# Layer 1's adaLN columns: weight tiles summed on VectorE in place of skinny matmuls on TensorE, in a two-layer trunk

## The chip, the cores and the metric

One core of a Trainium2 chip runs the whole program in one launch. The metric is the device time in microseconds (us) of one execution; lower is better. TensorE (PE in the profile) does the matmuls and transposes, VectorE (DVE) and ScalarE (ACT) the elementwise work, GpSimd (POOL) some of it, and SyncE (SP) issues the weight transfers.

## What is computed

A two-layer encoder trunk over 256 tokens of width 1024, in float32. Layer 0 is a pooling and S5 mixer, then a dense SwiGLU of hidden width 2816; layer 1 is a Mamba-2 mixer, then a top-2-of-8 expert SwiGLU. Each of the four sub-layers is framed by a modulation that comes from one conditioning vector c:

```
for layer in range(DEPTH):
    mod = (jax.nn.silu(c) @ ada_w[layer] + ada_b[layer])[:, None, :]
    sh_m, sc_m, g_m, sh_f, sc_f, g_f = jnp.split(mod, 6, axis=-1)
    h = _modulate(x, norm_g[layer, 0], sh_m, sc_m)
...
        y = _mamba2_mixer(h, m2_w_in[i], ...)
    x = x + g_m * _rmsnorm(y, norm_g[layer, 1])
    h = _modulate(x, norm_g[layer, 2], sh_f, sc_f)
...
```

`ada_w[layer]` is 1024x6144, so `silu(c) @ ada_w[layer]` is a product of one row with a 24 MB matrix, once per layer.

## The kernel before

**Tiles and order.** All weights stream through a ring of seven 2 MB slots, filled by SP in one fixed order (`plan`, L49) and freed by a counter, `tile_used`, that TensorE raises after the last use of each tile, in that same order. Each layer's `ada_w` is cut into 12 tiles (`NADA`) of 1024x512, held as 128 partitions x 8 chunks x 512 columns. Layer 0's twelve are used at the head of the program, layer 1's twelve are spread through the dense SwiGLU of layer 0.

**One ada tile before.** `ada_mm` (L1251) multiplies the eight chunks of the tile with the eight columns of silu(c) (`cT`) as 32-column weights, two chunks into each of four partition groups of bank 6; ScalarE's `ada` (L552) copies that bank to `modparts`; `ada_turn` (L1262) transposes it in four 128-column pieces into bank 7; VectorE's `mods` (L797) reduces the four groups and adds the bias, giving four columns of `mod`. So a tile goes TensorE, ScalarE, TensorE, VectorE, with one copy buffer and one bank at each step.

**The dense SwiGLU** (L1438 to L1465, and L674 and L972 on ScalarE and VectorE) runs six steps t. In step t TensorE computes, for each of four (two in the last step) groups of 128 hidden columns, a gate chain into bank 4 and an up chain into bank 5 of eight matmuls each; ScalarE takes silu of bank 4, VectorE multiplies it with bank 5 (`f_act`, L979). The next up chain may only start when that product has left bank 5. Then `ffn_down` of step t-1 adds into banks 0 to 3. Ada tiles are placed around these:

```
                if t < 5:
                    ada_turn(NADA + 2 * t + 1)
                pe.wait_ge(s["f_mm"], 8 * t + 2 * n_f)
                pe.sem_inc(s["tile_used"], 2)
                if t < 4:
                    ada_mm(NADA + 2 * t + 2)
                if t:
                    ffn_down(t - 1)
                if t < 4:
                    ada_turn(NADA + 2 * t + 2)
                    ada_mm(NADA + 2 * t + 3)
```

Tiles 0 and 1 of layer 1 are multiplied before the SwiGLU, between the end of the mixer's output projection and `turn_x(2)` (L1415 to L1419), tiles 10 and 11 behind it, before `turn_x(3)` (L1466 to L1473). These two places are boundaries between sub-layers: ScalarE squares the outputs (`y_squares`), VectorE forms the residual (`residual`) and the normalised x (`norm_x`), TensorE transposes it (`turn_x`, L1270), ScalarE and VectorE apply shift and scale (`hT_high`, `hT_low`), and the first chain of the next stage (`first_chain`, L1243) starts. At another such boundary, before the router, sixteen 128-column products of the identity (`stay_warm`, L1237) stand ahead of `turn_x(4)`. The first stage of layer 1 begins with one chain of eight matmuls and then 16 matmuls of only 32 columns (`dtw`, L1508).

Of the kernel before, what the change touches and what calls it, by code (L numbers as in the profile page):

```python
# [13 lines left out]
ALU = mybir.AluOpType  # L14
ACT = mybir.ActivationFunctionType
# [4 lines left out]
P = 128  # L20
D = 1024
KC = D // P
# [3 lines left out]
HALF = 512  # L26
# [22 lines left out]
def plan():  # L49

    tiles = []

    def put(kind, n, slot):
        tiles.append((kind, n, slot))

    head = [("ada0", n) for n in range(4)] + [("mixin", 1), ("mixin", 0)]
    head += [("ada0", n) for n in range(4, NADA)] + [("glu", 0), ("mixout", 0), ("mixout", 1)]
    for n, (kind, i) in enumerate(head):
        put(kind, i, n % S5_SLOTS)

    ada = [("ada1", n) for n in range(NADA)]
    ffn = ada[:2]
    for t in range(6):
        ffn += [("gate", t), ("up", t)]
        if t < 4:
            ffn.append(ada[2 * t + 2])
        if t:
            ffn.append(("down", t - 1))
        if t < 4:
            ffn.append(ada[2 * t + 3])  # L70
    ffn += [("down", 5)] + ada[10:]
    for n, (kind, i) in enumerate(ffn):
# [37 lines left out]
def hybrid_trunk(nc, a, out):  # L110
    with ExitStack() as ctx:
# [70 lines left out]
        def norm_col(layer, i):  # L182
# [20 lines left out]
        modparts = area(13312, HALF), area(18944, HALF)  # L203
# [60 lines left out]
            ada_copied ada_turned mod_ready inv_ready band_ready  # L264
# [276 lines left out]
        def _(act):  # L541
# [10 lines left out]
            def ada(i):  # L552

                act.wait_ge(s["tile_used"], ADA[i] + 1)
                if i:
                    act.wait_ge(s["ada_turned"], i)
                c.inc(f(modparts[i // NADA], ps[6][:, :], ACT.Copy), "ada_copied")
# [110 lines left out]
            ada(NADA)  # L668
            squares(1)
            ada(NADA + 1)  # L670
# [3 lines left out]
            for t in range(6):  # L674
                for j in range(2 if t == 5 else 4):
                    n = 4 * t + j
                    act.wait_ge(s["f_mm"], 2 * n + 1)
                    if n >= 2:
                        act.wait_ge(s["f_act"], n - 1)
                    c.inc(f(silu_f[:, n % 2], ps[4][:, 0:TOK], ACT.Silu), "f_silu")  # L680
                if t < 4:
                    ada(NADA + 2 * t + 2)
                    ada(NADA + 2 * t + 3)
            grow_rows(2, grow)
            y_squares(2)
            ada(2 * NADA - 2)
# [3 lines left out]
            ada(2 * NADA - 1)  # L690
            hT_high(3, NADA + 10, mod[:, 1, 0])
# [55 lines left out]
            hT_high(4, 2 * NADA, mod[:, 1, 3], hT2)  # L747
# [40 lines left out]
        def _(dve):  # L788
# [8 lines left out]
            def mods(i):  # L797

                dve.wait_ge(s["ada_turned"], i + 1)
                m = modraw[:, i % 2]  # L800
                c.then(v.tensor_reduce(m, bank(7, 4, 4, 32)[:, :, :, 0], AX.X, ALU.add), step)
                layer, n = i // NADA, i % NADA
                at = layer * 48 + 4 * n
                c.inc(tt(mod_flat[:, at:at + 4], m, cols[:, 0, at:at + 4], ALU.add), "mod_ready")

# [160 lines left out]
            mods(NADA)  # L966
# [21 lines left out]
            mods(2 * NADA - 2)  # L988
            scale_cols(3, NADA + 10, mod[:, 1, 1], norm_col(1, 0))
            hT_low(3, mod[:, 1, 0])  # L990
            mods(2 * NADA - 1)
# [95 lines left out]
            scale_cols(4, 2 * NADA, mod[:, 1, 4], norm_col(1, 2))  # L1087
# [135 lines left out]
        def _(pe):  # L1223
# [38 lines left out]
            def ada_turn(i):  # L1262
# [3 lines left out]
                for k in range(4):  # L1266
                    ins = turn(ps[7][:, P * k:P * k + P], modparts[i // NADA][:, P * k:P * k + P], ident[:, :])
# [147 lines left out]
            ada_mm(NADA)  # L1415
            ada_turn(NADA)
            ada_mm(NADA + 1)
# [20 lines left out]
            for t in range(6):  # L1438
# [20 lines left out]
                if t < 4:  # L1459
                    ada_turn(NADA + 2 * t + 2)  # L1460
                    ada_mm(NADA + 2 * t + 3)
# [4 lines left out]
            ada_mm(2 * NADA - 2)  # L1466
            ada_turn(2 * NADA - 2)
            ada_mm(2 * NADA - 1)
# [4 lines left out]
            ada_turn(2 * NADA - 1)  # L1473
# [19 lines left out]
            for n in range(32):  # L1493
# [10 lines left out]
                if n == 0:  # L1504
                    pe.wait_ge(s["l1_in"], 96)
                    pe.wait_ge(s["ada_copied"], 2 * NADA)
# [19 lines left out]
            pe.wait_ge(s["mod_ready"], 2 * NADA)  # L1526
# [267 lines left out]
```

## Time and profile before

| | us |
|---|---|
| median of 3 runs | 1730.05 |
| lowest and highest | 1729.53, 1731.7 |
| the profiled execution | 1730.87 |
| its span | 1729.0 |
| TensorE busy in it | 1563.1 |
| VectorE busy in it | 389.0 |
| granted TensorE clock, mean | 0.972 of full speed |

The span is the time from the first to the last instruction of the profiled execution; its own time is 1.9 us longer. "Granted clock" is the share of TensorE's full speed that the chip gave; it has two levels, 1.00 (2.4 GHz) and 0.50 (1.2 GHz).

The order of the main stages in the span: the layer 0 mixer ends at 201 us, the dense SwiGLU runs from 209.6 to 461 us, the Mamba-2 stage starts at 470 us, the experts fill the last 930 us.

### The profile page before, as it was taken

To read this page: it belongs to the slowest core of one execution; us is meant where nothing else is said; L and a number is where in the kernel's file an instruction comes from. 1 tells how busy PE (TensorE), PEld (TensorE's weight loads), DVE (VectorE), ACT (ScalarE), POOL (GpSimd) and SP (SyncE) were. 2 spreads that over 40 slices of the span, in tenths; PEclk is the share of its full clock that TensorE was granted. 3 is DMA by queue.
4 is the path that set the end of the run, shared out by engine and by line. 5 is a ranking of instruction groups with operands and counts; after the bars stand their busy time and mean duration, and the time that the engine had idled before them with its cause. 6 is when DMAs were issued, how large, how long until landed. Compare 5 with 4: busy or idle time off the path is not lost.

```text
span 1729.0 us, 24503 instructions
## 1 busy us (share of the span) xinstructions
PE 1563.1 (90%) x10777; PEld 898.4 (52%) x10778; DVE 389.0 (23%) x846; ACT 219.7 (13%) x419; POOL 106.3 (6%) x129
## 2 busy tenths in 40 slices
PE   7886999999999999988999999999979979877876
PEld 5654486667588766554333353356646643423322
DVE  5796200000255555131010001010010010100102
ACT  2411300000321143220000000000000000000001
POOL 6164000000000011000000000000000000000000
PEclk8998999999999999988999999999989989999999
DMA  9476396642464404434999887999979969999996
GB/s 335 160 245 245 143 352 257 241 171 100 164 226 147 146 1 147 146 146 167 404 409 409 314 292 305 403 408 407 403 270 371 378 249 402 405 409 403 408 408 245
DMA packets 167299, 485.78 MB, mean 281 GB/s; under 512 B 12928, under 2 KB 15872, under 8 KB 167168
## 3 DMA queue, kind: packets, MB, share of 16 engines
q1 hardware_dynamic: 162624, 482.51, 73.4%
q8 instruction: 106, 1.74, 0.4%
q10 hardware_dynamic: 4544, 1.33, 0.4%
q14 instruction: 25, 0.20, 0.0%
HBM read 482.78 MB, written 1.05 MB: 280 GB/s over the span
## 4 chain that ended last, share of the span: by engine, by line
PE 73%; DMA 11%; DVE 6%; issue 5%; SPq 3%; ACT 1%; POOL 0%; DVEq 0%; POOLq 0%; ACTq 0%
PE bank L1694 23%; PE bank L1234 20%; PE bank L1725 10%; DMA ring<-in_moe_w_down 7%; PE bank L1429 4%; PE bank L1619 3%; DMA ring<-in_moe_w_up 3%; SPq L439 3%; PE bank L1539 2%; PE bank L1671 2%; DMA ring<-in_moe_w_gate 1%; PE bank L1259 1%; DVE arena L941 1%; PE bank L1241 1%; PE bank L1578 1%
## 5 line engine op out<-in xcount | busy, mean ns | idle before, releaser
L1694 PE MATMUL bank<-ring,arena 128*32 128x256 f32 (+3 forms) x4864 | 506.5, 428 | 72.9 <-issue 45.7
L1694 PEld LDWEIGHTS bank<-ring,arena 128*32 128x32 f32 (+1 forms) x4864 | 231.3, 121 | 337.1 <-issue 262.8
L1234 PE MATMUL bank<-arena,ring 128*128 128x256 f32 x1264 | 283.8, 384 | 1.3 <-ACT arena L646 1.0
L1725 PE MATMUL bank<-ring,arena 128*32 128x256 f32 (+1 forms) x2128 | 249.9, 459 | 29.9 <-DMA ring<-in_moe_w_down 27.6
L1234 PEld LDWEIGHTS bank<-arena,ring 128*128 128x128 f32 x1264 | 241.2, 193 | 38.9 <-issue 4.5
L1725 PEld LDWEIGHTS bank<-ring,arena 128*32 128x32 f32 (+1 forms) x2128 | 101.6, 120 | 168.1 <-issue 118.6
L1159 DVE TENSOR_TENSOR arena<-arena,bank 128x512 f32<-128x512 f32 (+2 forms) x44 | 24.4, 577 | 606.8 <-PE bank L1694 606.8
L763 ACT ACTIVATE arena<-bank 128x512 f32<-128x512 f32 (+2 forms) x44 | 21.1, 508 | 692.3 <-PE bank L1706 576.0
L1429 PE MATMUL bank<-ring,arena 128*128 128x512 f32 x176 | 77.0, 595 | 0.3 <-PE bank L1234 0.3
L1539 PE MATMUL bank<-ring,arena 128*128 128x512 f32 x128 | 59.3, 606 | 2.5 <-DVE hd L1055 2.5
L1619 PE MATMUL bank<-ring,arena 128*128 128x512 f32 x128 | 55.3, 592 | 0.0
L1429 PEld LDWEIGHTS bank<-ring,arena 128*128 128x128 f32 x176 | 33.0, 190 | 42.5 <-issue 42.4
L1259 PE MATMUL bank<-ring,cT 128*32 128x512 f32 x384 | 48.0, 618 | 3.1 <-DMA ring<-in_ada_w 2.5
L1173 DVE TENSOR_TENSOR arena<-arena,bank 128x512 f32<-128x512 f32 x32 | 22.0, 688 | 108.7 <-PE bank L1671 107.9
L979 DVE TENSOR_TENSOR arena<-arena,bank 128x256 f32<-128x256 f32 x22 | 9.3, 422 | 164.4 <-PE bank L1234 164.4
L503 POOL TENSOR_TENSOR arena<-arena,ring 128x512 f32<-128x512 f32 x32 | 41.5, 1316 | 70.1 <-DVE arena L949 62.8
L1145 DVE TENSOR_SCALAR arena<-bank,gs,mod 128x128 f32<-128x128 f32 x64 | 21.9, 404 | 95.5 <-PE bank L1234 95.5
L528 POOL COPY arena<-arena 128x6 f32<-128x6 f32 x8 | 1.5, 190 | 669.2 <-DVE arena L1136 649.2
L1234 PE MATMUL bank<-ring,arena 128*128 128x512 f32 x96 | 42.0, 594 | 0.1
L518 POOL TENSOR_TENSOR arena<-arena,hd 128x256 f32<-128x256 f32 x16 | 10.2, 638 | 515.9 <-ACT arena L700 388.2
L1619 PEld LDWEIGHTS bank<-ring,arena 128*128 128x128 f32 x128 | 24.2, 190 | 29.7 <-issue 29.7
L1539 PEld LDWEIGHTS bank<-ring,arena 128*128 128x128 f32 x128 | 23.7, 196 | 26.8 <-issue 26.8
(262 smaller groups left out, 1122.9 us busy)
## 6 DMA issues: line engine op xcount, KB each, us to landing
ring<-in_moe_w_gate SPq DMA_DIRECT2D x56, 2048.0 KB, 21.5
ring<-in_moe_w_up SPq DMA_DIRECT2D x56, 2048.0 KB, 22.3
ring<-in_moe_w_down SPq DMA_DIRECT2D x56, 2048.0 KB, 19.3
ring<-in_ada_w SPq DMA_DIRECT2D x24, 2048.0 KB, 11.1
ring<-in_m_w_in SPq DMA_DIRECT2D x12, 2048.0 KB, 8.5
ring<-in_ffn_w_gate SPq DMA_DIRECT2D x5, 2048.0 KB, 16.5
ring<-in_ffn_w_up SPq DMA_DIRECT2D x5, 2048.0 KB, 12.4
ring<-in_ffn_w_down SPq DMA_DIRECT2D x5, 2048.0 KB, 7.9
```

The source lines that it names most:

```text
L439: sp.dma_start(dst, src.rearrange("e p k n -> p (e k) n")).then_inc(ring_full[j % RING], 16)
L503: c.inc(g.tensor_tensor(qq[:, q % 2, k], zz[:, q % 2], tables[:, 1 - k, q:q + 1, :].broadcast_to([P, 2, TOK]), ALU.mult), "q_ready")
L1159: ins = tt(sg[:, b, 0:w], sg[:, b, 0:w], ps[2 + b][:, 0:w], ALU.mult)
L1173: tt(o, o, ps[SCATTER[i]][:, :], ALU.add).then_inc(s["acc_done"], 1)
L1234: ins = mm(out_, l, r, start=i == 0, stop=i == len(pairs) - 1, **kw)
L1259: ins = mm(ps[6][32 * j:32 * j + 32, :], cT[:, kc, :], w[:, kc, :], start=half == 0, stop=half == 1)
L1429: ins = mm(ps[i][:, :], act_f[:, t % 2, j, P * b:P * b + P], w[:, j, HALF * h:HALF * h + HALF], start=t == 0 and j == 0, stop=t == 5 and j ...
L1539: ins = mm(ps[6 + zi % 2][:, :], hT[:, kc, P * b:P * b + P], w[:, kc], start=kc == 0, stop=kc == KC - 1)
L1619: ins = mm(ps[4 + i][:, :], yT1[:, 4 * t + j, P * b:P * b + P], w[:, j, HALF * h:HALF * h + HALF], start=t == 0 and j == 0, stop=t == 3 an ...
L1671: mm(ps[SCATTER[i]][:, :], gates[:, P * (i // 2):P * (i // 2) + P], y_sb[:, HALF * (i % 2):HALF * (i % 2) + HALF], start=True, stop=True). ...
L1694: ins = mm(ps[base + b // per][m * h:m * h + m, w * (b % per):w * (b % per) + w], hcur3[:, kc, m * b:m * b + m], sl[:, kc - half * rows, w ...
L1725: ins = mm(ps[4 + b // per][m * h:m * h + m, w * (b % per):w * (b % per) + w], actT[:, t % 2, b // per, n * (b % per) + i, m * q:m * q + m ...
```

## The change

Layer 1's twelve ada tiles no longer go through `ada_mm` and `ada_turn`. VectorE forms, for each tile, the sum over its eight chunks of the chunk times its column of silu(c) (one `tensor_scalar` and seven `scalar_tensor_tensor` operations over 128x512, each waiting for the one before) into one of two buffers, `modsum`. TensorE sums that over the partitions with four matmuls per tile, each with 128 columns of `modsum` as weights and one column of ones as the moving operand, into four columns of bank 7, and frees the tile. After the twelfth tile VectorE adds the bias to all 48 columns at once. ScalarE has no part in it any more. All twelve tiles now lie inside the six steps of the SwiGLU, two per step, and the load order is changed to fit.

```diff
-    ffn = ada[:2]
+    ffn = []
     for t in range(6):
-        ffn += [("gate", t), ("up", t)]
-        if t < 4:
-            ffn.append(ada[2 * t + 2])
+        ffn += [("gate", t), ("up", t), ada[2 * t]]
         if t:
             ffn.append(("down", t - 1))
-        if t < 4:
-            ffn.append(ada[2 * t + 3])
-    ffn += [("down", 5)] + ada[10:]
+        ffn.append(ada[2 * t + 1])
+    ffn.append(("down", 5))
...
+            def sum_rows(n, first):
+
+                o = modsum[:, n % 2]
+                i = AT["ada1", n]
+                w = slot(TILES[i][2], KC, HALF)
+                if first == 0:
+                    dve.wait_ge(ring_full[TILES[i][2]], 16 * FILL[i])
+                    if n >= 2:
+                        dve.wait_ge(s["tile_used"], AT["ada1", n - 2] + 1)
+                for kc in range(first, first + 4):
+                    if kc == 0:
+                        c.then(ts(o, w[:, 0], cT[:, 0, 0:1], None, ALU.mult), step)
+                    else:
+                        c.then(stt(o, w[:, kc], cT[:, kc, 0:1], o, ALU.mult, ALU.add),
+                               "ada_summed" if kc == KC - 1 else step)
...
                     c.inc(tt(act_f[:, t % 2, j], silu_f[:, n % 2], ps[5][:, 0:TOK], ALU.mult), "f_act")
-                if t < 5:
-                    mods(NADA + 2 * t + 1)
-                if t < 4:
-                    mods(NADA + 2 * t + 2)
+                    if t < 5:
+                        sum_rows(2 * t + j // 2, 4 * (j % 2))
+                    else:
+                        sum_rows(10, 4 * j)
+            sum_rows(11, 0)
+            sum_rows(11, 4)
+            dve.wait_ge(s["tile_used"], AT["ada1", NADA - 1] + 1)
+            c.inc(tt(mod_flat[:, 48:96], ps[7][:, 0:48], cols[:, 0, 48:96], ALU.add), "mod_ready")
             residual(2, 12, 2, grow)
...
-            ada_mm(NADA)
-            ada_turn(NADA)
-            ada_mm(NADA + 1)
+            def ada_columns(n):
+
+                pe.wait_ge(s["ada_summed"], n + 1)
+                for k in range(4):
+                    ins = mm(ps[7][:, 4 * n + k:4 * n + k + 1], modsum[:, n % 2, P * k:P * k + P], ones[:, 0:1],
+                             start=True, stop=True)
+                ins.then_inc(s["tile_used"], 1)
...
-                if t < 5:
-                    ada_turn(NADA + 2 * t + 1)
                 pe.wait_ge(s["f_mm"], 8 * t + 2 * n_f)
                 pe.sem_inc(s["tile_used"], 2)
-                if t < 4:
-                    ada_mm(NADA + 2 * t + 2)
+                ada_columns(2 * t)
                 if t:
                     ffn_down(t - 1)
-                if t < 4:
-                    ada_turn(NADA + 2 * t + 2)
-                    ada_mm(NADA + 2 * t + 3)
+                ada_columns(2 * t + 1)
...
             ffn_down(5)
-            ada_mm(2 * NADA - 2)
-            ada_turn(2 * NADA - 2)
-            ada_mm(2 * NADA - 1)
 
             pe.wait_ge(s["x_ready"], 4)
             turn_x(3)
-            ada_turn(2 * NADA - 1)
```

ScalarE loses its `ada` copies of layer 1, and the waits on `mod_ready` behind the SwiGLU now wait for the one addition.

TensorE, from the mixer's output projection (L1234 before, L1242 now, 128x512 x32) to the third step of the SwiGLU; `first_chain` is L1248 before and L1256 now, `turn_x` L1275 and L1283, gate and up chains the 128x256 rows, `ffn_down` L1429 and L1442. Before:

```order
L1234 MATMUL bank<-ring,arena 128x512 x32
L1259 MATMUL bank<-ring,cT 32x512 x8
L1267 MATMUL bank<-ident,arena 128x128 x4
L1259 MATMUL bank<-ring,cT 32x512 x8
L1275 MATMUL bank<-ident,arena 128x128 x16
L1248 MATMUL bank<-arena,ring 128x256 x8
L1234 MATMUL bank<-arena,ring 128x256 x56
L1267 MATMUL bank<-ident,arena 128x128 x4
L1259 MATMUL bank<-ring,cT 32x512 x8
L1267 MATMUL bank<-ident,arena 128x128 x4
L1259 MATMUL bank<-ring,cT 32x512 x8
L1234 MATMUL bank<-arena,ring 128x256 x64
```

And now, with `ada_columns` at L1427:

```order
L1242 MATMUL bank<-ring,arena 128x512 x32
L1283 MATMUL bank<-ident,arena 128x128 x16
L1256 MATMUL bank<-arena,ring 128x256 x8
L1242 MATMUL bank<-arena,ring 128x256 x56
L1427 MATMUL bank<-ones,arena 128x1 x8
L1242 MATMUL bank<-arena,ring 128x256 x64
L1427 MATMUL bank<-ones,arena 128x1 x4
L1442 MATMUL bank<-ring,arena 128x512 x16
L1427 MATMUL bank<-ones,arena 128x1 x4
```

Nothing stands between the projection and `turn_x` any more, and the eight one-column matmuls of the first step (two tiles) follow each other directly.

VectorE in the last step of the SwiGLU, now; L985 is the product `f_act`, L808 and L810 are `sum_rows`, L993 the addition of the bias, L848 the start of the residual:

```order
L985 TENSOR_TENSOR arena<-arena,bank 128x256
L808 TENSOR_SCALAR arena<-ring,cT 128x512
L810 SCALAR_TENSOR_TENSOR arena<-ring,cT,arena 128x512 x3
L985 TENSOR_TENSOR arena<-arena,bank 128x256
L810 SCALAR_TENSOR_TENSOR arena<-ring,cT,arena 128x512 x4
L808 TENSOR_SCALAR arena<-ring,cT 128x512
L810 SCALAR_TENSOR_TENSOR arena<-ring,cT,arena 128x512 x7
L993 TENSOR_TENSOR mod<-bank,cols 128x48
L848 TENSOR_TENSOR arena<-bank,arena 128x512 x3
```

The second half of tile 10's sum stands behind the last product, and tile 11's whole sum behind that; in every other step one half of a sum stands behind each product.

## Rows read from the trace of the kernel before

**Rows 1.** The page: busy us, share of the span and instructions.

```profile
PE 1563.1 (90%) x10777; PEld 898.4 (52%) x10778; DVE 389.0 (23%) x846; ACT 219.7 (13%) x419; POOL 106.3 (6%) x129
```

**Rows 2.** The chain that ended last, in the SwiGLU: start us, us, what.

```profile
213.31 24.17 PE bank L1234 x112
...
243.00 27.82 PE bank L1234 x128
...
273.12 13.93 PE bank L1429 x32
...
382.01 27.82 PE bank L1234 x128
410.27 13.84 PE bank L1429 x32
424.11 13.83 PE bank L1234 x64
438.23 13.97 PE bank L1429 x32
```

**Rows 3.** The timeline at the mixer's end, ScalarE: start us, us, instruction, idle before.

```profile
203.18 0.60 ACT L557 ACTIVATE arena<-bank 128x512 f32<-128x512 f32 x1 [1.03 <-PE bank L1259]
...
203.84 1.06 ACT L564 ACTIVATE arena<-x 128x1024 f32<-128x1024 f32 x1
```

**Rows 4.** The timeline of VectorE: a product, then scalar_tensor_tensor pairs of two widths.

```profile
237.52 0.42 DVE L979 TENSOR_TENSOR arena<-arena,bank 128x256 f32<-128x256 f32 x1 [6.49 <-PE bank L1234]
...
462.48 2.48 DVE L849 SCALAR_TENSOR_TENSOR x<-arena,rst,x 128x1024 f32<-128x1024 f32 x2
...
481.05 1.00 DVE L1017 SCALAR_TENSOR_TENSOR arena<-bank,cols,arena 128x255 f32<-128x255 f32 x2
```

**Rows 5.** Groups by line and shape, VectorE: count | busy us, mean ns.

```profile
L1027 DVE TENSOR_TENSOR arena<-arena 128x512 f32<-128x512 f32 x16 | 10.9, 680 | 0.0
```

**Rows 6.** The timeline of TensorE: 32-column products, chains, and turn_x at two places.

```profile
206.52 2.30 PE L1275 MATMUL bank<-ident,arena 128*128 128x128 f32 x16 [0.17 <-DVE arena L811]
...
473.67 3.74 PE L1234 MATMUL bank<-dtw,arena 128*128 128x32 f32 x32
477.22 8.77 PE L1234 MATMUL bank<-arena,ring 128*128 128x256 f32 x32
...
486.05 3.62 PE L1234 MATMUL bank<-arena,ring 128*128 128x256 f32 x16
...
763.63 3.49 PE L1275 MATMUL bank<-ident,arena 128*128 128x128 f32 x16 [2.96 <-DVE arena L811]
```

**Rows 7.** Stretches: length, PE, PEld, DVE, ACT, POOL busy (count), granted clock, DMA, GB/s.

```profile
115.30:118.70 3.40, 1.54 (x12) 0.68 (x4) 3.33 (x7) 0.60 (x1) 1.68 (x2) 1.00 1.04 389
118.70:122.10 3.40, 3.00 (x9) 2.60 (x10) 3.30 (x6) 0.00 (x0) 2.19 (x3) 0.50 1.05 393
...
147.70:151.00 3.30, 0.00 (x0) 0.01 (x1) 3.23 (x7) 0.60 (x1) 1.63 (x3) 1.00 0.55 204
151.00:156.20 5.20, 2.42 (x12) 1.73 (x12) 5.06 (x10) 0.42 (x1) 3.12 (x3) 1.00 0.00 0
156.30:166.40 10.10, 6.76 (x16) 4.91 (x16) 1.93 (x4) 2.08 (x3) 1.90 (x2) 0.50 0.80 280
201.20:206.50 5.30, 4.43 (x36) 1.32 (x37) 4.23 (x7) 3.91 (x10) 0.00 (x0) 1.00 0.82 279
461.20:466.40 5.20, 4.39 (x36) 1.26 (x36) 4.23 (x7) 3.81 (x10) 0.00 (x0) 1.00 0.84 275
473.70:477.10 3.40, 3.40 (x33) 3.40 (x31) 0.00 (x0) 0.00 (x0) 0.00 (x0) 1.00 1.05 385
477.10:480.50 3.40, 3.40 (x10) 2.77 (x10) 1.04 (x6) 2.42 (x4) 0.00 (x0) 0.50 1.05 388
...
763.90:767.10 3.20, 3.20 (x16) 2.81 (x14) 0.51 (x2) 0.00 (x0) 0.00 (x0) 0.50 1.03 417
```

**Rows 8.** SP's timeline, then the DMA issues of 100 to 480 us with median landing.

```profile
201.43 3.85 SPq L404 DMA_DIRECT2D ring<-in_ada_w  x2
...
ring<-in_ada_w SPq DMA_DIRECT2D x15, 2048.0 KB, 12.8
```

More of the change, by code:

```diff
@@ L202, in hybrid_trunk @@
         grow = area(13312, D)
-        modparts = area(13312, HALF), area(18944, HALF)
+        modpart = area(13312, HALF)
+        modsum = area(8192, 2, HALF)
         temps = area(14336, 2, 2, 2, TOK)
@@ L263, in hybrid_trunk @@
         names = """small_in x_in step_in s5_in c_in pw_in l1_in consts t_iota rows_turned cols_ready cT_zero c_ready
-            ada_copied ada_turned mod_ready inv_ready band_ready
+            ada_copied ada_turned ada_summed mod_ready inv_ready band_ready
             step_exp step_ready mag_ready inv_tail turn_ready turn_sin tab_ready tab_sin bx_zero bx_ready b_turned bt_ready c_turned ct_zero ct_ready
@@ L556, in ada @@
                     act.wait_ge(s["ada_turned"], i)
-                c.inc(f(modparts[i // NADA], ps[6][:, :], ACT.Copy), "ada_copied")
+                c.inc(f(modpart, ps[6][:, :], ACT.Copy), "ada_copied")
             def squares(n):
@@ L667, in _ @@
             y_squares(1)
-            ada(NADA)
             squares(1)
-            ada(NADA + 1)
             hT_high(2, NADA, mod[:, 0, 3])
@@ L680, in _ @@
                     c.inc(f(silu_f[:, n % 2], ps[4][:, 0:TOK], ACT.Silu), "f_silu")
-                if t < 4:
-                    ada(NADA + 2 * t + 2)
-                    ada(NADA + 2 * t + 3)
             grow_rows(2, grow)
             y_squares(2)
-            ada(2 * NADA - 2)
             squares(2)
-            ada(2 * NADA - 1)
-            hT_high(3, NADA + 10, mod[:, 1, 0])
+            hT_high(3, NADA + 1, mod[:, 1, 0])
             act.wait_ge(s["l1_in"], 96)
@@ L746, in _ @@
             squares(3)
-            hT_high(4, 2 * NADA, mod[:, 1, 3], hT2)
+            hT_high(4, NADA + 1, mod[:, 1, 3], hT2)
             act.wait_ge(s["rt_pre"], 1)
@@ L965, in _ @@
             norm_x(2)
-            mods(NADA)
             scale_cols(2, NADA, mod[:, 0, 4], norm_col(0, 2))
@@ L979, in _ @@
                     c.inc(tt(act_f[:, t % 2, j], silu_f[:, n % 2], ps[5][:, 0:TOK], ALU.mult), "f_act")
-                if t < 5:
-                    mods(NADA + 2 * t + 1)
-                if t < 4:
-                    mods(NADA + 2 * t + 2)
+                    if t < 5:
[6 more added lines that the diff above has]
+            c.inc(tt(mod_flat[:, 48:96], ps[7][:, 0:48], cols[:, 0, 48:96], ALU.add), "mod_ready")
             residual(2, 12, 2, grow)
             norm_x(3)
-            mods(2 * NADA - 2)
-            scale_cols(3, NADA + 10, mod[:, 1, 1], norm_col(1, 0))
+            scale_cols(3, NADA + 1, mod[:, 1, 1], norm_col(1, 0))
             hT_low(3, mod[:, 1, 0])
-            mods(2 * NADA - 1)
             gate_cols(3, mod[:, 1, 2], norm_col(1, 1))
@@ L1084, in _ @@
             residual(3, 20, 4, grow1, 4, True)
-            scale_cols(4, 2 * NADA, mod[:, 1, 4], norm_col(1, 2))
+            scale_cols(4, NADA + 1, mod[:, 1, 4], norm_col(1, 2))
             norm_x(4)
@@ L1266, in ada_turn @@
                 for k in range(4):
-                    ins = turn(ps[7][:, P * k:P * k + P], modparts[i // NADA][:, P * k:P * k + P], ident[:, :])
+                    ins = turn(ps[7][:, P * k:P * k + P], modpart[:, P * k:P * k + P], ident[:, :])
                 ins.then_inc(s["ada_turned"], 1)
@@ L1450, in _ @@
                         ins.then_inc(s["f_mm"], 1)
-                if t < 5:
-                    ada_turn(NADA + 2 * t + 1)
                 pe.wait_ge(s["f_mm"], 8 * t + 2 * n_f)
                 pe.sem_inc(s["tile_used"], 2)
-                if t < 4:
-                    ada_mm(NADA + 2 * t + 2)
+                ada_columns(2 * t)
                 if t:
                     ffn_down(t - 1)
-                if t < 4:
-                    ada_turn(NADA + 2 * t + 2)
-                    ada_mm(NADA + 2 * t + 3)
+                ada_columns(2 * t + 1)
             pe.wait_ge(s["gg_ready"], 2)
@@ L1505, in _ @@
                     pe.wait_ge(s["l1_in"], 96)
-                    pe.wait_ge(s["ada_copied"], 2 * NADA)
+                    pe.wait_ge(s["ada_copied"], NADA)
                     for b in range(NB):
@@ L1524, in _ @@
                     ins.then_inc(s["cs_mm"], 1)
-            pe.wait_ge(s["mod_ready"], 2 * NADA)
+            pe.wait_ge(s["mod_ready"], NADA + 1)
             def z_part(n):
```

## The prediction

> **What bounds the kernel now.** I read the page first: TensorE is busy 90% of the span, VectorE 23% [rows 1]. Then the chain that ended last, since busy shares say nothing of a stage. Inside the dense SwiGLU that chain is TensorE alone: chains, down products and, between them, the ada work, each starting where the last ends [rows 2]. So there an ada tile costs what it takes on TensorE, and VectorE has long idle stretches (6.49 us before each product [rows 4]). At the two boundaries around the SwiGLU the chain runs through ScalarE and VectorE instead, and TensorE's ada work fits in their shadow. Last I read the granted clock in short stretches, because the change takes work off TensorE exactly where it is not the bound [rows 7].
>
> After the SwiGLU everything is shifted by whatever is gained or lost: the ring is only seven tiles deep and SP loads in order, so the experts' transfers start later or earlier by the same amount. I carry the sum unchanged to the end.
>
> **The sum with the clock at full speed.** Price of a one-column set: four matmuls, two passes each in float32. The nearest row is the 32-column product, 32 passes in 3.55 us from 473.67 to 477.22 [rows 6], 0.111 us a pass, bound by loading 128 columns of weights: 8 x 0.111 = 0.89 us. Bounds: 0.8 to 1.0.
>
> Price of one step of the sum on VectorE, 128x512: two 1024-column operations take 2.48 us together, two 255-column ones 1.00 [rows 4], so 1.24 and 0.50 per step are the ends; a two-source 512-column operation takes 0.680 [rows 5]. I take 0.72 with the wait for the step before. Half a tile is then 2.9 us. It fits the 6.49 us idle behind each product, so the next product, and TensorE's next up chain, are not late; it would take 1.6 us a step for that.
>
> - *Step 0.* Before, the chain ends at 213.31 + 24.17 = 237.48 and the next starts at 243.00 [rows 2]: 5.52 us for two turns, two ada products and a wait for ScalarE's copy. Now tile 0's columns (0.89) run while VectorE finishes tile 1, whose second half stands behind the product: 0.46 for the product, 2.88 for four steps, 0.1 for the signal, then 0.89: 4.3 us. Gain 1.2.
> - *Steps 1 to 3.* Before, 243.00 + 27.82 = 270.82 to 273.12 [rows 2], 2.3 us, six times. Now 0.89 six times; the sum behind `ffn_down` is long done (13.9 us cover it). Gain 6 x 1.41 = 8.4.
> - *Step 4.* Before, 409.83 to 410.27, 0.44 us, and nothing at 424.11 [rows 2]. Now two sets, 1.78. Loss 1.3.
> - *Step 5.* Before, 437.94 to 438.23, 0.29 us [rows 2]. Now TensorE waits for tile 10's second half, which stands behind the last product: 0.46 + 2.88 + 0.1 + 0.89 = 4.3. Loss 4.0. Tile 11 is summed under `ffn_down(4)`; its columns cost 0.9.
> - *Boundaries.* ScalarE's copy ended at 203.78 and its squares began at 203.84, when the residual's first half was just ready [rows 3]; removing the copy is worth at most 0.06. The other pieces lie under the transposes. Gain 0.
> - *Loads.* The order is gate 0, up 0, ada 0 into the three slots free early, then ada 1, issued near 201.4 where two ada tiles are issued now [rows 8]. It is wanted by VectorE at about 231; even at twice the 12.8 us to landing [rows 8] it is there. Later tiles have more time. Cost 0. VectorE waiting for a tile would hold the product queued behind it and so TensorE; that is a rival.
> - *The bias* is added under the last down products; the residual follows later. Cost 0.
>
> Sum: -1.2 - 8.4 + 1.3 + 4.0 + 0.9 = **-3.4 us**.
>
> **The clock.** Today TensorE is busy 4.43 of 5.30 us at the first boundary and 4.39 of 5.20 at the second, and the clock stays at 1.00 [rows 7]. Most of that is the ada work; without it TensorE stands idle for over 5 us at each. What such idling does is shown elsewhere: 3.30 idle us from 147.7 were followed by thin work at 1.00 and then by 10.1 us at 0.50; a stretch of 3.40 us with TensorE busy 1.54 was enough for 0.50 in the next [rows 7]. And thin matmuls don't hold it: TensorE was busy all of 473.7 to 477.1 with 32-column products, and had 0.50 from 477.1 [rows 6, 7]. So I expect it to fall at both boundaries, and at the two new waits (steps 0 and 5), where for over 4 us there is nothing but waiting and one-column matmuls.
>
> Prices: `turn_x` takes 3.49 us at 0.50 against 2.30 at 1.00 [rows 6]: 1.2, all on the chain. Chains: 32 passes across the half-speed stretch took 8.77 us, where 16 take 3.62 and the next 16 add about 3.5: 1.7 lost [rows 6].
> - First boundary: 1.2 plus a little of the first chain, 1.4.
> - Second: the same 1.2, but the fall at 477.1 is paid already, and the new one may replace or precede it: 0.6 (ends 0 and 2.9).
> - Each wait: up to 1.7 on the chains behind it, and the one-column matmuls slower, 0.9 at most; 2.0 each, 4.0.
>
> That is +6.0, and the whole **+2.6 us**: 1730.87 for the profiled execution becomes 1733.5. That execution lies 0.8 above the median of the runs, 1730.05, so the median becomes **1732.6**. The ends: all stays at full speed, -3.4; or every fall costs both turns and chains, below.
>
> The Trainium skill, page "TensorE: Matmul & The Clock Gate", section "Why this matters for your kernels", advises against idle gaps between bursts of matmuls because the engine drops back to half clock. By that rule the change gives back its gain, sum +2.6; without it the sum is -3.4. The trace agrees where it shows such gaps (0.50 after the stretches above).
>
> **Rivals.**
> *A. The clock holds.* The idling at the boundaries doesn't pull it down, or the half-speed stretch falls into the wait itself, where it costs nothing. For it: after 147.7 to 151.0, wholly idle, the clock stayed at 1.00 for 5.2 us more [rows 7]. Against it: it then fell. Time: 1730.05 - 3.4 = 1726.7. Chance 0.15.
> *B. Half speed lasts.* At each of the four places the clock comes back only after more than one stretch, as after 156.3 (10.1 us at 0.50 with TensorE busy 6.76 [rows 7]). Each boundary then costs 1.2 + 1.7 and each wait 0.9 + 1.7: 11.0 - 3.4 = +7.6, 1737.7, slower. It decides once the falls cost over 6.9 us together (3.4 given back and 0.2% on top). For it: work is thin on both sides of each wait. Against it: behind 477.1 to 480.5 the chains ran at full speed again [rows 6]. Chance 0.20.
> *C. VectorE is held by a load.* A sum waits for its tile, the next product stands behind it, and TensorE with it. It decides when a tile lands more than 29 us after its issue at 201.4; in the later steps, after more than some 20 us. At 1 us a tile, +12 less the 3.4: about 1739, slower. Against it: 12.8 us to landing [rows 8]. Chance 0.03.
> *D. The steps are cheaper or dearer.* At 0.50 a step both waits are 0.9 shorter and the clock may hold there: about 1728; at 1.24, each 2.1 longer and 1737. Chance 0.07.
> *E. The change doesn't do what it says*: the order of instructions shows eight and four one-column matmuls at the places named, and none of the old ones; chance 0.
>
> **How the numbers follow.** The forecast, falls at three or four places at the prices above, has 0.55, between about 1729.5 and 1735.5 as the stretches fall. 0.2% of 1730.05 is 3.5 us, about what a measurement of this kernel can tell from no change: 1726.6 and 1733.5. Faster: nearly half of A and a little of D, 0.10. Slower: B, C, half of D and a fifth of the forecast's own spread, 0.38. Same: the rest, 0.52. The range, 1727.0 to 1737.0, leaves out the lower half of A and the upper half of B, with C.
>
> **What would show it.** Right: TensorE's waits of 2 to 3 us for `ada_summed` in steps 0 and 5 and nowhere else; 0.9 us between chain and down product in steps 1 to 4; steps of 0.72 us on VectorE; `turn_x` at about 3.5 us at both boundaries; four stretches at 0.50 between 200 and 480 us instead of one. Wrong: a clock at 1.00 behind the boundaries; a product of the SwiGLU that starts late; one-column sets far from 0.9 us; or a difference that arises among the experts.

## The result, and the profile after

| | before | after |
|---|---|---|
| median of 5 runs, us | 1730.05 | 1739.84 |
| lowest and highest | 1729.53, 1731.7 | 1736.44, 1743.0 |
| the profiled execution | 1730.87 | 1743.0 |
| its span | 1729.0 | 1740.8 |
| granted clock, mean | 0.972 | 0.962 |

Against the kernel before in the same session the ratio is 1.0052, with a 95% interval from 1.004 to 1.0065. The change costs 9.8 us by the medians and 11.8 by the two spans: the profiled execution of the changed kernel is the slowest of its five, 3.2 us above their median, so what is read from its trace comes out somewhat larger than in the medians. The forecast was 1732.6, in a range up to 1737.0.

The busy totals of the changed kernel, from its page, answer to [rows 1]:

```profile
PE 1557.9 (89%) x10633; PEld 904.0 (52%) x10634; DVE 453.0 (26%) x919; ACT 212.8 (12%) x407; POOL 106.2 (6%) x129
```

TensorE is busy 5.2 us less and yet the span is 11.8 us longer, so TensorE stands idle 17 us more. I look for it stage by stage. The offset is the start of the same instruction after, less the same before:

| place | before | after | offset |
|---|---|---|---|
| end of the mixer's projection | 200.91 | 199.37 | -1.5 |
| first chain of the SwiGLU | 209.62 | 209.42 | -0.2 |
| first chain of layer 1 | 470.14 | 473.26 | +3.1 |
| second chain behind the 32-column products | 486.21 | 487.65 | +1.4 |
| `turn_x(4)` | 763.63 | 765.15 | +1.5 |
| the gather for the first expert, behind the router | 784.96 | 787.09 | +2.1 |
| first expert | 795.63 | 800.86 | +5.2 |
| scatter inside the fourth expert | 1147.70 | 1159.64 | +11.9 |
| end of span | 1729.0 | 1740.8 | +11.8 |

So from the projection to 487.65 the local loss is 3.0 us, where the forecast said 2.6. The head of the program, which the change doesn't touch, ran 1.5 us faster in this execution. Nearly all of the rest arises at two places among the experts, some 340 and 690 us behind the last changed instruction. Behind them the offset still moves both ways (the stop at the entry to the fifth expert is 12.30 us before, from 1262.50, and 10.67 after, from 1275.82, with an offset of 13.3 ahead of it), but it ends where it was.

**The two places.** The chain that ended last, before, at the entry to the experts and in the fourth expert (start us, us, what; "issue" is time with nothing to wait for):

```profile
789.02 1.79 PE bank L1241 x16
790.81 4.83 issue
795.63 9.47 PE bank L1694 x29
...
1134.34 2.79 issue
1137.13 10.57 PE bank L1694 x192
1147.70 3.63 PE bank L1671 x8
```

The same of the changed kernel:

```profile
791.14 1.79 PE bank L1249 x16
792.93 7.92 issue
800.86 4.53 PE bank L1698 x9
...
1139.45 2.73 issue
1142.18 1.02 PE bank L1698 x11
1143.21 4.53 issue
1147.73 11.91 PE bank L1698 x181
1159.64 3.63 PE bank L1675 x8
```

At the entry "issue" grows from 4.83 to 7.92, 3.1 us. In the fourth expert the 192 matmuls (as the profile counts them, see below) that ran as one block of 10.57 us now stop after 11 for 4.53 us. The other 181 take 11.91 us, where their share of the 10.57 is 9.96, since the granted clock fell to 0.50 in the middle of the stop. It is 0.50 in the whole of this window, columns as in [rows 7]:

```profile
1144.70:1151.30 6.60, 3.56 (x36) 1.72 (x40) 0.00 (x0) 0.00 (x0) 0.00 (x0) 0.50 1.02 407
```

Together it is 20.19 us in place of 13.36, 6.8 more. Nothing in these pieces waits for a semaphore, an engine or a weight tile.

**Where instructions come from.** Section 3 of the page has a queue that brings instructions, in both kernels the same:

```profile
q8 instruction: 106, 1.74, 0.4%
```

Its packets are of 16384 bytes; they are called blocks here. These are the starts of the loads around the two places (each took 0.9 to 1.2 us). That they are TensorE's is read from their times, which go with its stops:

```
kernel     entry to the experts        fourth expert
before     793.09  796.20              1134.48  1140.27
after      795.36  798.35  801.89      1139.53  1145.24
```

**The changed stretch.** The chain in steps 0, 1 and 5 of the SwiGLU, changed kernel; L985 is the product, L810 `sum_rows`, L1427 the columns, L1442 `ffn_down`:

```profile
213.12 24.19 PE bank L1242 x112
...
237.38 0.42 DVE arena L985
...
240.08 0.76 DVE arena L810
...
240.88 1.86 PE bank L1427 x8
242.75 29.84 PE bank L1242 x128
...
272.72 1.02 PE bank L1427 x8
273.75 13.84 PE bank L1442 x32
287.59 0.79 PE bank L1427 x8
...
418.98 13.94 PE bank L1242 x64
...
432.99 0.42 DVE arena L985
...
436.49 1.05 PE bank L1427 x8
437.54 15.54 PE bank L1442 x32
453.08 0.79 PE bank L1427 x8
```

Against [rows 2]: step 0 has 5.44 us between its chain and the next (5.52 before), but the columns take 1.86 in it and the chain behind 29.84 instead of 27.82. In step 1 the columns take 1.02 and 0.79. In step 5 TensorE waits: from 432.92 to 437.54 there are 4.62 us, and the down products behind take 15.54 where they took 13.97.

The windows of the changed kernel at the boundaries and the two waits, columns as in [rows 7]:

```profile
199.40:202.40 3.00, 0.00 (x0) 0.00 (x0) 2.25 (x5) 1.08 (x4) 0.00 (x0) 1.00 0.56 141
202.50:209.30 6.80, 3.65 (x16) 3.28 (x16) 3.44 (x8) 3.22 (x8) 0.00 (x0) 0.50 1.05 396
240.10:246.80 6.70, 5.92 (x18) 5.11 (x19) 0.73 (x1) 0.00 (x0) 0.00 (x0) 0.50 1.02 407
438.10:441.40 3.30, 3.30 (x5) 1.22 (x5) 3.16 (x5) 0.00 (x0) 0.00 (x0) 0.50 0.81 243
465.40:472.10 6.70, 3.65 (x16) 3.27 (x16) 3.33 (x8) 2.94 (x7) 0.00 (x0) 0.50 1.05 387
```

The clock falls to 0.50 (1.2 GHz) at both boundaries and at both waits, each time behind a stretch in which TensorE did nothing or little.

### The profile page after: what moved, and what is told of

It is laid out like the page before. It is cut to its first block, busy times and chain, and to the rows that moved or that the text cites. A ratio compares the mean times of both kernels' runs of the same rounds, so it can differ in the third digit from the quotient of the medians.

```text
span 1740.8 us, 24255 instructions
## 1 busy us (share of the span) xinstructions
PE 1557.9 (89%) x10633; PEld 904.0 (52%) x10634; DVE 453.0 (26%) x919; ACT 212.8 (12%) x407; POOL 106.2 (6%) x129
## 3 DMA queue, kind: packets, MB, share of 16 engines
q10 hardware_dynamic: 4544, 1.33, 0.4%
## 4 chain that ended last, share of the span: by engine, by line
PE 74%; DMA 11%; DVE 7%; issue 5%; SPq 2%; ACT 1%; POOL 0%; DVEq 0%; POOLq 0%; ACTq 0%
PE bank L1698 23%; PE bank L1242 21%; PE bank L1729 11%; DMA ring<-in_moe_w_down 8%; PE bank L1442 4%; PE bank L1623 3%; DMA ring<-in_moe_w_up 3%; PE bank L1543 2%; SPq L437 2%; PE bank L1675 2%; DVE arena L948 1%; PE bank L1249 1%; PE bank L1710 1%; PE bank L1582 1%; DVE arena L956 1%
## 5 line engine op out<-in xcount | busy, mean ns | idle before, releaser
L1242 PE MATMUL bank<-arena,ring 128*128 128x256 f32 x1264 | 284.3, 385 | 1.3 <-ACT arena L644 1.0
L1242 PEld LDWEIGHTS bank<-arena,ring 128*128 128x128 f32 x1264 | 241.4, 193 | 35.3 <-ACT arena L644 1.7
L1442 PE MATMUL bank<-ring,arena 128*128 128x512 f32 x176 | 78.6, 605 | 0.0
L810 DVE SCALAR_TENSOR_TENSOR arena<-ring,cT,arena 128x512 f32<-128x512 f32 x84 | 63.1, 751 | 2.6
L1442 PEld LDWEIGHTS bank<-ring,arena 128*128 128x128 f32 x176 | 33.6, 193 | 40.3 <-issue 40.3
L985 DVE TENSOR_TENSOR arena<-arena,bank 128x256 f32<-128x256 f32 x22 | 9.3, 421 | 152.8 <-PE bank L1242 152.8
L1242 PE MATMUL bank<-ring,arena 128*128 128x512 f32 x96 | 42.0, 594 | 0.1
```

Of the source, the lines that this page charges most:

```text
L810: c.then(stt(o, w[:, kc], cT[:, kc, 0:1], o, ALU.mult, ALU.add), "ada_summed" if kc == KC - 1 else step)
L1242: ins = mm(out_, l, r, start=i == 0, stop=i == len(pairs) - 1, **kw)
L1442: ins = mm(ps[i][:, :], act_f[:, t % 2, j, P * b:P * b + P], w[:, j, HALF * h:HALF * h + HALF], start=t == 0 and j == 0, stop=t == 5 and j ...
```

## The experiments

The theory, P (place of the code): the change is worth about +1 to +3 us by itself; the rest, near 8, comes from the 312 instructions less, wherever they are. Its rival (timing): the experts stall because the changed order makes something there late, and where the code lies does nothing. All kernels ran in five rounds against the kernel before. Only TensorE's program is filled in them, so the code of the other engines stays where it is.

**1. The old place, by filling.** Into the changed kernel go 56 instructions that do nothing but count up a semaphore, which makes 256 less than before, a whole block.

```diff
+            def pad_code(n):
+                for _ in range(n):
+                    pe.sem_inc(s["pad"], 1)
+
+            pad_code(56)
             pe.wait_ge(s["x_ready"], 2)
             turn_x(2)
```

> The changed kernel plus 56 one-instruction semaphore increments on TensorE in the idle time before turn_x(2). Same work; but every expert's code on TensorE then starts at the same place within a 16 KB block of code as in the kernel before (56 is what 312 instructions fewer lack to 256). Theory P (code position): the two stalls that grew, before the first expert's first matmul (7.9 us against 4.8) and inside the fourth expert's first tile (4.5 us after 11 matmuls, then half clock), go back to the old values; time 1731 to 1734 instead of 1739.8. Rival T (the experts start late for another reason: the loads or the clock set them off differently after an earlier or later start): stalls and time stay, 1738 to 1742.

Measured: 1737.41, ratio 1.0042 (1.0028 to 1.0057), profiled 1736.85: the expected 1731 to 1734 was missed, and the rival's 1738 to 1742 nearly reached. In the profile both stalls are back to before's (5.10 us at the entry, none inside the fourth expert). But `turn_x(2)` starts at 208.25 instead of 204.97: the 56 instructions took longer than the gap that I had put them in. So both stalls went as the theory says, but the time settles nothing here; experiment 4 repeats it with the filling elsewhere.

**2. The kernel before, moved.** The other way round: 200 such instructions in the S5 mixer of the kernel before, 13 or 14 in each of 15 turns of a loop. 200 more is the same place in a block of 256 as 56 less, and so as 312 less.

```diff
             for q in range(NQ):
...
+                if q >= 1:
+                    pad_code(14 if q < 6 else 13)
```

> The kernel before plus 200 one-instruction semaphore increments on TensorE, 13 or 14 in each step of the S5 loop, where TensorE has slack behind VectorE. No part of the change is in it, but the experts' code then starts at the place in a 16 KB block that it has in the changed kernel. Theory P: the stalls appear here too, some 3 us at the first expert and 4.5 plus half clock at the fourth; the start of the dense SwiGLU moves by at most 2 us; time 1738 to 1742. Rival T: no new stall, 1730 to 1732.

Measured: 1738.05, ratio 1.0045 (1.0031 to 1.0059): the kernel before, with not one changed matmul, has lost 7.4 us. Its chain:

```profile
790.07 8.20 issue
...
1136.99 2.74 issue
1139.73 1.02 PE bank L1702 x11
1140.76 4.64 issue
1145.40 11.81 PE bank L1702 x181
```

The same 11 matmuls, a stop of 4.64 us, the same 181 slow ones. The SwiGLU starts at 209.52 (209.62 before), so the filling cost nothing where it lies, and the last scatter comes 9.05 us later (1725.23 against 1716.18). The rival has nothing to explain it with: no order, load or sum is changed here.

One more thing in this trace bears on the clock. The prediction read from [rows 6, 7] that 32-column products don't hold it, because it was at 0.50 behind 477.1. Here the same products of the same kernel, at the same time, are followed by full speed:

```profile
473.60:477.00 3.40, 3.40 (x33) 3.40 (x31) 0.00 (x0) 0.00 (x0) 0.00 (x0) 1.00 1.06 389
477.10:480.50 3.40, 3.40 (x18) 3.01 (x18) 1.22 (x6) 2.60 (x4) 0.00 (x0) 1.00 1.05 383
```

So it is in the trace of experiment 3. The fall at 477.1 belongs to the one execution of [rows 7], not to the code before.

**3. A dose between.** 100 instead of 200, so that the fourth expert's code begins at place 134 and its next block is needed after (256 - 134) / 2 = 61 passes.

```diff
+                if q >= 1:
+                    pad_code(6 + (10 >= q))
```

> The kernel before plus 100 pad instructions in the S5 loop. Theory P, graded by position: the first expert's code begins 153 instructions into its block, far from the end, so its start is as before (4.8 us); the fourth's begins about 134 in, with 122 left, some 3.4 us of its quick 256-column products, where the next block took 5.5 us from the start to come: a stall of about 2 us in it, against 0 before and 4.6 with 200. Time 1732 to 1735. If only the amount of padding cost, half of e2's loss: 1734, with no stall inside the fourth expert.

Measured: 1733.67, ratio 1.0016 (1.0004 to 1.0028), profiled 1731.11. The chain in the fourth expert:

```profile
1131.94 2.72 issue
1134.66 3.65 PE bank L1702 x61
1138.31 2.08 issue
1140.39 7.53 PE bank L1702 x131
```

The stop stands after the 61st matmul and is 2.08 us long: the later the block is needed, the shorter the wait for it (4.53 after 11, 2.08 after 61, none before). At the entry there are 4.88 us, as before. The time alone would also fit filling that costs by its amount (half of experiment 2's loss is 1734); the place and length of the stop, told ahead, don't.

**4. The change at before's code place, filling where it is free.** The changed kernel with the 56 in the S5 loop.

```diff
+                if q >= 1:
+                    pad_code(3 + (11 >= q))
```

> As e1, but the 56 pad instructions stand in the S5 loop, where 200 of them cost nothing in e2, and not in the idle time before turn_x(2), where they delayed it by 3.3 us in e1. Theory P: e1 less those 3.3 us: 1733 to 1735, that is 4 us over the kernel before, from the waits and the clock in the SwiGLU and at its boundaries. If padding is not free there, or e1's time had another source: 1737 or more.

Measured: 1731.91 (12 runs), ratio 1.0006 (0.9997 to 1.0015), below the expected 1733 to 1735. Its chain at the two places:

```profile
791.52 4.93 issue
796.45 6.93 PE bank L1706 x17
...
1135.11 2.69 issue
1137.81 10.57 PE bank L1706 x192
```

Adding 56 instructions that do nothing takes 7.9 us off the median (1739.84 to 1731.91; by the ratios to the kernel before, 1.0052 to 1.0006, it is 8.0). What the change itself does is then +1 us, not to be told from nothing. In the traces the place costs more than in the medians: the offset from the gather ahead of the first expert to the end is 9.7 us after against before (11.8 less 2.1) and 9.8 in experiment 2, where the medians lose 7.9 and 7.4. The traced executions of these two kernels lie 3.2 and 1.8 us above their medians, that of before 0.8.

**5. Is it the clock at the boundaries?** Five 512-column products of the identity ahead of each `turn_x`, as the router has them (`stay_warm`), fill the gap that the ada work left; 16 instructions more keep the code at before's place (the ten products are 40).

```diff
+            for _ in range(5):
+                mm(ps[6][:, :].rearrange("p (a b) -> p a b", a=4), ident[:, :],
+                   ones[:, :].unsqueeze(1).broadcast_to([P, 4, P]), start=True, stop=True)
```

> The changed kernel with five 512-column products of the identity (20 instructions) in the idle time before turn_x(2), five more before turn_x(3), and 16 pad instructions, so that the code position is that of the kernel before. Theory P and clock: turn_x back to 2.3 us at both boundaries from 3.65, no half-speed stretch there; against e1 it saves 1.3 us at the first and 0 to 2.5 at the second: 1729 to 1732. If idling at the boundaries is not what pulls the clock down, turn_x stays at 3.65 us and the time is that of e1.

Measured, with the 16 directly ahead of the first five: 1731.77, ratio 1.0008 (0.9999 to 1.0016). `turn_x(2)` starts only at 209.59, pushed by the filling as in experiment 1.

With the 16 in the S5 loop instead:

> The changed kernel with two buffers and its waits as they are, five 512-column products of the identity at each boundary, and 16 pad instructions in the S5 loop (20 + 20 + 16 = 56, the code position of the kernel before). Against e5 this takes the falls at the boundaries away and nothing else: turn_x 2.3 us at both, 2.5 us less up to the first chain of layer 1, and up to 1.7 more where the 32-column products pulled the clock down: 1727.5 to 1730. If the boundaries' falls cost nothing, 1732 as e5.

Measured: 1732.43 (12 runs), ratio 1.0009 (0.9998 to 1.002): expected up to 1730, missed. TensorE's timeline shows both turns at full speed:

```profile
204.86 2.31 PE L1283 MATMUL bank<-ident,arena 128*128 128x128 f32 x16 [0.94 <-DVE arena L818]
...
468.18 2.30 PE L1283 MATMUL bank<-ident,arena 128*128 128x128 f32 x16 [0.94 <-DVE arena L818]
```

So idling did bring the half clock there, and products in the gap prevent it: 3.65 became 2.31 and 2.30, 2.7 us on the chain. Yet the median is that of experiment 4. In the profiled execution the fall in step 5 lasted 6.8 us instead of 3.4, and there is one at 478.5, as before the change had one at 477.1. Whether that is where the 2.7 went in the other eleven runs no trace tells; it stays open.

**6. Without the two waits.** Four `modsum` buffers instead of two, and each tile's columns half a step later: tile 2t-1 ahead of `ffn_down(t-1)`, tile 2t behind it, tile 11 last. The load order follows.

```diff
-        ffn += [("gate", t), ("up", t), ada[2 * t]]
+        ffn += [("gate", t), ("up", t)]
         if t:
-            ffn.append(("down", t - 1))
-        ffn.append(ada[2 * t + 1])
+            ffn += [ada[2 * t - 1], ("down", t - 1)]
+        ffn.append(ada[2 * t])
+    ffn.append(ada[11])
...
-        modsum = area(8192, 2, HALF)
+        modsum = area(8192, 4, HALF)
...
-                ada_columns(2 * t)
                 if t:
+                    ada_columns(2 * t - 1)
                     ffn_down(t - 1)
-                ada_columns(2 * t + 1)
+                ada_columns(2 * t)
+            ada_columns(NADA - 1)
```

With the 56 ahead of `turn_x(2)`, to compare with experiment 1:

> The changed kernel with four buffers for the sums instead of two, each odd tile's columns one step later (before the down products of the next step) and tile 10's and 11's behind ffn_down(4), and 56 pad instructions. TensorE then never waits for a sum in steps 0 and 5. Theory: both waits (2.4 and 3.6 us) and the half-speed stretches behind them (2 us each) go, TensorE's path in the SwiGLU is shorter by 9 to 11 us than in e1: 1721 to 1725. If the sums on VectorE are late after all, or the loads in the new order, a wait for ada_summed or a load shows and less than half of that is gained.

Measured: 1723.79, ratio 0.9965 (0.9954 to 0.9976), 13.6 us below experiment 1. VectorE now waits 59.6 us in all for ada tiles, and TensorE never waits for a sum. From its first chain to the end of its last down products the SwiGLU takes 242.55 us, and 253.13 in experiment 1.

With the 56 in the S5 loop, to compare with experiment 4:

> As e4 (four buffers, columns a step later), with the pad in the S5 loop. Theory: e4 less 3.3 us: 1719.5 to 1722. turn_x still 3.65 us at both boundaries, as the clock falls there.

Measured: 1723.46, ratio 0.9951 (0.9934 to 0.9968), above the expected 1719.5 to 1722, and 8.5 us below experiment 4. The waits of steps 0 and 5 with the half clock behind them are worth 8.5 us by this pair of medians, 13.6 by the other; the traces of the two pairs show 10.4 and 10.6 less from the first chain of the SwiGLU to that of layer 1.

**7. Both.** Experiment 6 with the five products at each boundary and 16 instructions of filling in the S5 loop.

> As e6 with five 512-column products of the identity at the head of the idle time at each boundary (and 16 pad instructions in the S5 loop for 56). Theory of the clock: no half-speed stretch between 200 and 209 us nor at the end of the SwiGLU before the 32-column products; turn_x 2.3 us; 1.2 to 3 us under e6: 1717 to 1720. Rival: the clock falls anyway behind the boundaries (the 32-column products at the second do it) and only the first is gained, 1 us.

Measured: **1714.81** (1712.63 to 1718.12), ratio 0.9908 (0.9892 to 0.9923), below both kernels and below what was expected. Its chain in steps 0 and 5:

```profile
234.88 0.14 issue
235.01 1.02 PE bank L1436 x8
...
424.24 1.02 PE bank L1436 x8
425.27 13.84 PE bank L1454 x32
```

The 0.14 and 1.02 us are all that stands between the chains in step 0, where it was 5.44. The timeline of TensorE at the first boundary (L1441 the wide products, L1284 `turn_x`):

```profile
198.42 4.53 PE L1441 MATMUL bank<-ones,ident 128*128 128x512 f32 x10
...
203.90 2.30 PE L1284 MATMUL bank<-ident,arena 128*128 128x128 f32 x16 [0.94 <-DVE arena L819]
```

The down products of step 5 take 13.84 again (15.54 with the wait). Against experiment 6 the traces show the first chain 1.3 us earlier (207.00, 208.31), layer 1's 2.7 (458.83, 461.49), `turn_x(4)` 4.4 (749.23, 753.58), the last scatter 5.6 (1703.19, 1708.79). The first 2.7 are the two turns. The next 1.7 come with a half-speed stretch that the other has from 586.5 to 589.9 us and this one has not: between 163.3 and 750.4 us its clock is never at 0.50. The medians differ by 8.7, more than these traces, and the traced execution of experiment 7 is the slowest of its six. The same ten products gave nothing by the medians in experiment 5 (1731.91 and 1732.43), so what they are worth here is not settled.

**8. The best one, moved.** Experiment 7 with 216 instructions of filling instead of 16, the changed kernel's place in the block.

```diff
-                    pad_code(1 + (1 >= q))
+                    pad_code(14 + (6 >= q))
```

> e7, the fastest so far, with 216 pad instructions in the S5 loop instead of 16: the experts' code in the changed kernel's position. Theory P: the same two stalls as in the changed kernel and in e2 (8 us before the first expert, 4.5 us inside the fourth) come back on the same work: 7 to 10 us over e7's 1714.8, so 1722 to 1725. If the position mattered only together with the old clock falls, 1715 to 1718.

Measured: 1727.4, ratio 0.9983 (0.9974 to 0.9991), 12.6 us above experiment 7, more than expected. The stops are at the known places (7.72 us at the entry; 4.53 after 11 matmuls, then 181 in 11.87). In the traces some 3 us lie ahead of the SwiGLU (first chain at 209.97, not 207.00); whether the filling or the start of the program made them was not separated (with equal filling and the same code ahead, the projection ends at 199.2 in experiment 5's second trace and at 198.3 in experiment 7's).

## Why the prediction was wrong

**The step that failed** is the one with no sum in it: "After the SwiGLU everything is shifted by whatever is gained or lost", "I carry the sum unchanged to the end". It took a fixed program behind the change for granted and asked only about loads of weights. But the change also shortens TensorE's program, and all branch targets behind move in their blocks. Costed from what the runs show, that term is +3.1 at the entry and +6.8 in the fourth expert by the two traces, or 7.9 us by the medians of experiment 4. With it, 2.6 + 7.9 is 10.5, and 9.8 was measured. The trace of before showed the place: 4.83 and 2.79 us of "issue" at branches, with nothing awaited. The forecast rests on no row of the experts at all. "A difference that arises among the experts" stood at the end of the prediction as what would make it wrong, but with no price and no chance, so the range didn't hold it.

**The local sum, term by term**, changed kernel against before:
- *Step 0.* Said: gain 1.2, then a fall of 2.0. Measured 5.44 against 5.52, and 29.84 against 27.82 behind: loss 1.9 where 0.8 was forecast. The step of the sum was 0.76 long, not 0.72, and the columns 1.86, not 0.89, at half clock. I had named that doubling within the 2.0, and it came on top.
- *Steps 1 to 3.* Said -8.4. Sets of 1.16 (with 0.14 of issue) and 0.79, mean 0.97: 6 x 1.33 = -8.0. Right, the set a little undersized.
- *Step 4.* Said +1.3; 1.16 + 0.79 - 0.44 = +1.5.
- *Step 5.* Said +4.0, +0.9 and a fall of 2.0. Measured 4.62 - 0.29 = +4.3, +0.8, and 15.54 - 13.97 = +1.6. Right, to 0.2 together.
- *Boundaries.* Said +1.4 and +0.6. The first is 10.05 us from projection to first chain against 8.71, +1.34. The second is 10.62 against 9.27, +1.35, less 1.7 as the half-speed stretch of 477.1 [rows 7] is gone: -0.35. That 1.7 is luck and no gain of the change: the stretch is missing in two traces of the unchanged work as well (experiments 2 and 3). "Thin matmuls don't hold it" was wrongly read from one execution. `turn_x` takes 3.65 at both, said "about 3.5". Four stretches at 0.50 in place of one, as forecast.
- *Loads, bias.* Right at zero: no product is late, TensorE waits for `ada_summed` in steps 0 and 5 alone.

These come to +3.0 (1.3 - 0.4 + 1.9 - 8.0 + 1.5 + 6.7) against +2.6, or to +4.7 without the luck of the 1.7, so the closeness is in part chance. Experiment 4 shows it at the end of the program as +1 us by the medians, with an interval from -0.5 to +2.6 (0.9997 and 1.0015 of 1730.8). The head's 1.5 us and 0.6 us between 765 and 787 belong to this one execution as far as the runs show; the 0.6 was not followed.

**The rivals.** A (the clock holds) is refuted by four windows at 0.50. B (half speed lasts) was half right: three of the four stretches lasted 6.8 us and one 3.4. But only step 0 cost what B says (2.0 on the chain and about 0.9 on the columns); each boundary cost 1.3 where B has 2.9, and step 5 1.6 where it has 2.6. Together that is 7.2 us, between the forecast's 6.0 and B's 11.0. C: no load was late. D: 0.76 us a step. That the time lies where B and C put it (1737.7 and 1739) is no support for them; experiment 2 reaches 1738.05 with no part of the change in it. So the rule on idle gaps (the Trainium skill, "TensorE: Matmul & The Clock Gate", section "Why this matters for your kernels") was rightly weighed and agrees with the windows, but it explains some 6 us that the sum already had, not the 8 that were missing.

## What to carry to other kernels

When a change adds or removes instructions on an engine that later branches, the cost can lie at the branches, hundreds of us away and with no semaphore involved: look in the trace of before for "issue" behind a branch, count the instructions added or removed modulo a block of 256, and price another place in the block at what the trace gives. To judge the change itself, compare it at the same place (fill where the engine's wait is long and elsewhere free), or two variants differ by 8 us that neither of them earned. The fastest kernel here has that place in it too: of its gain against before, 0.9%, only 0.2% is left at the changed kernel's place (experiment 8). Work that is taken off TensorE in the shadow of another engine costs nothing there before and gives nothing after, but may have held its clock: order sums so that TensorE never waits for them, which was worth 8.5 us at an equal place, the surest gain here. Wide products in the gap kept the clock up in all three traces that have them in a free gap, but showed in the medians of only one of two pairs.

## What the runs showed of the hardware

- At the branch into the fourth expert TensorE stops for 2.7 to 2.8 us in every trace while a block loads, and the next block's load starts 5.7 to 5.9 us after the first. At the entry to the experts the stop is 4.8 to 5.4 us; about 2.3 of it pass before the load starts (790.81 to 793.09 before), and what they are wasn't separated. Code that begins 22 instructions ahead of its block's end stops again for 4.5 us; 122 ahead, for 2.1; 222 ahead, not at all (all in the fourth expert).
- The stop drags the clock down with it: in all three kernels with the stop after 11 matmuls (the changed one, experiments 2 and 8) the clock falls to 0.50 some 1.3 us into the stop and stays there for 6.8 us. Behind the 2.08 us stop of experiment 3 it stayed at 1.00.
- 56 semaphore increments on TensorE cost 3.3 us on the path (208.25 against 204.97) although the engine stood idle there for over 5 us: TensorE is idle for 8.84 us there, which makes an estimate of 0.16 us each. The 16 of experiment 5's first kernel took 2.60, again 0.16 each. Such an instruction is not free in a gap of that size.
- One scalar_tensor_tensor over 128x512, each waiting for the one before, takes 0.751 us, from the groups by line of the changed kernel:

```profile
L810 DVE SCALAR_TENSOR_TENSOR arena<-ring,cT,arena 128x512 f32<-128x512 f32 x84 | 63.1, 751 | 2.6
```
